# The latent gate's two GEMMs between the latents' projections, norms and queries of a two-block kernel; the first convolution's GEMM inside the attention loop

## What is computed

```python
z, xbc, dt_raw, q_a, c_kv, k_rope, gate_ssd, gate_mla = split_cols(u @ w_in[i], IN_SPLITS)
y_ssd = ssd_branch(z, xbc, dt_raw, ...) @ w_ssd_out[i]      # begins with a causal convolution of xbc and a SiLU
y_mla = mla_branch(q_a, c_kv, k_rope, ...) @ w_mla_out[i]   # latent attention, 16 heads
merged = jax.nn.sigmoid(gate_ssd) * y_ssd + jax.nn.sigmoid(gate_mla) * y_mla
```

```python
q = (rms_norm_2(q_a, q_a_norm) @ w_q_b).reshape(b, s, MLA_HEADS, QK_HEAD_DIM)
kv = (rms_norm_2(c_kv, kv_a_norm) @ w_kv_b).reshape(b, s, MLA_HEADS, QK_NOPE_DIM + V_HEAD_DIM)
```

## Time and profile before

| quantity | value |
|---|---|
| median of 3 runs | 1200.77 us (1197.71 to 1200.79) |
| the profiled execution's own time | 1201.91 us |
| its span in the trace | 1199.8 us |
| mean granted TensorE clock in it | 0.945 of full |
| PE busy | 1058.1 us, 88% of the span |
| POOL, DVE, ACT busy | 651.6, 532.0, 428.1 us |

### The profile page before, as it was taken

The page is one execution under the profiler, slowest core; times in us unless marked ns, Lnnn a source line. Parts: engine busy times, 40 slices in busy tenths (PEclk is TensorE's granted clock), DMA queues, the critical chain, the costliest instruction groups (busy, mean ns, idle before and its releaser), DMA issues.

```text
span 1199.8 us, 18315 instructions
## 1 busy us (share of the span) xinstructions
PE 1058.1 (88%) x7022; PEld 865.8 (72%) x7022; DVE 532.0 (44%) x1199; ACT 428.1 (36%) x641; POOL 651.6 (54%) x535
## 2 busy tenths in 40 slices
PE   5897899987957979999999999999985899999990
PEld 4786888987947879999976879898964555544440
DVE  6303246368545665644169886841226311111113
ACT  4543333332325546554434444354422211111111
POOL 5997814356738676664755359888540122322221
PEclk9999898999987889999998999999997999999996
DMA  6454522333424344432433226555425699999983
GB/s 255 174 200 166 183 71 71 113 117 123 141 105 142 139 141 141 141 137 75 164 126 102 100 72 212 175 176 175 176 105 246 219 417 418 417 417 419 418 338 110
DMA packets 35598, 229.05 MB, mean 191 GB/s; under 512 B 6320, under 2 KB 6320, under 8 KB 8768
## 3 DMA queue, kind: packets, MB, share of 16 engines
q1 hardware_dynamic: 30672, 220.07, 48.9%
q0 software_dynamic: 3696, 4.21, 1.1%
q10 hardware_dynamic: 1152, 3.67, 0.9%
HBM read 246.79 MB, written 11.27 MB: 215 GB/s over the span
## 4 chain that ended last, share of the span: by engine, by line
POOL 44%; issue 31%; DMA 11%; PE 11%; DVE 3%; POOLq 1%; ACT 0%; DVEq 0%
POOL wlo L516 44%; DMA ring<-in_experts 10%; PE ps L2320 5%; PE ps L2334 3%; DMA yg<-expert_rows,posn 1%; PE ps L2307 0%; PE ps L2282 0%; PE ps L1744 0%; PE ps L2283 0%; PE ps L1746 0%; PE ps L1745 0%; DVE xlo L983 0%; POOLq L519 0%; DVE over L1703 0%; DVE x L1718 0%
## 5 line engine op out<-in xcount | busy, mean ns | idle before, releaser
L516 POOL TENSOR_TENSOR wlo<-raw,whi 128x512 fp32r<-128x512 f32 x448 | 583.5, 1338 | 308.4 <-ACT whi L574 307.9
L1794 PE MATMUL ps<-xhi,whi 128*128 128x256 f32 x960 | 283.8, 296 | 10.5 <-DVE xlo L1200 4.1
L1795 PE MATMUL ps<-xhi,wlo 128*128 128x256 f32 x960 | 277.9, 289 | 0.0
L1796 PE MATMUL ps<-xlo,whi 128*128 128x256 f32 x960 | 277.7, 289 | 0.0
L574 ACT ACTIVATE whi<-raw 128x2048 fp32r<-128x2048 f32 x112 | 213.9, 1914 | 146.9 <-PE ps L1796 75.5
L1794 PEld LDWEIGHTS ps<-xhi,whi 128*128 128x128 f32 x960 | 191.3, 199 | 14.7 <-issue 7.2
L1795 PEld LDWEIGHTS ps<-xhi,wlo 128*128 128x128 f32 x960 | 190.9, 199 | 1.0 <-issue 0.7
L1796 PEld LDWEIGHTS ps<-xlo,whi 128*128 128x128 f32 x960 | 190.7, 199 | 0.0
L2320 PE MATMUL ps<-ring,xw 128*64 128x256 f32 x1248 | 152.6, 385 | 8.4 <-DMA ring<-in_experts 6.2
L2320 PEld LDWEIGHTS ps<-ring,xw 128*64 128x64 f32 x1248 | 86.8, 137 | 69.0 <-issue 29.5
L541 POOL DMA_INDIRECT expert_rows<-yb,dest x39 | 38.6, 989 | 172.4 <-ACT yb L900 172.4
(11 more groups left out here) (451 smaller groups left out, 1435.3 us busy)
## 6 DMA issues: line engine op xcount, KB each, us to landing
ring<-in_experts SPq DMA_DIRECT2D x117, 1024.0 KB
raw<-in_weights SPq DMA_DIRECT2D x112, 1024.0 KB, 4.9
x<-in_x SPq DMA_DIRECT2D x2, 512.0 KB, 4.6
memt<-in_mem ACTq DMA_DIRECT2D x1, 1024.0 KB, 6.1
out<-xn ACTq DMA_DIRECT2D x4, 256.0 KB, 2.5
expert_rows<-yb,dest POOLq DMA_INDIRECT x39
decay<-in_decay ACTq DMA_DIRECT2D x1, 512.0 KB, 3.6
npost<-in_norm_post ACTq DMA_DIRECT2D x1, 512.0 KB, 5.1
```

Of the source, the lines that this page charges most:

```text
L516: ins = pool.tensor_tensor(wlo[:, j, c], raw[:, j, c], whi[:, j, c].bitcast(f32), ALU.subtract)
L1794: mm(o_, wh[:, k, cc], hi[:, k0 + r0 + k, :], start=first, stop=False, skip_group_check=True)
L1795: mm(o_, wl[:, k, cc], hi[:, k0 + r0 + k, :], start=False, stop=False, skip_group_check=True)
L1796: ins = mm(o_, wh[:, k, cc], lo[:, k0 + r0 + k, :], start=False, stop=last, skip_group_check=True)
```

## The change

`gm0` and `gm1` move from the end of the attention's filler to the stretch behind `pb`: PE runs `gm0` (two units) ahead of the wait for `qa_ready`, and `gm1` (two units) behind the transposes of `ck` and `kp`. `xbc0` leaves that stretch and becomes the first two units of the filler, which now has twelve units (u from 0 to 11) and nothing behind the loop. The convolution's instructions of ACT and DVE move one odd or even iteration on, so that `conv_taps(5)` stands in u = 11 and `conv_silu(5)` in u = 12. `pa` and `pb` get another place in SBUF, since the gate's result `gmT` now exists while they do. No instruction is added or removed.

```diff
@@ unit_plan
     add("pb", w, 1024, r(5536, 5824))
-    add("xbc0", w, 1024, r(2048, 2560))
+    for i in range(2):
+        add(f"gm{i}", w, 1024, r(6848 + 512 * i, 7360 + 512 * i))
...
-    for i in range(1, 6):
+    for i in range(6):
         add(f"xbc{i}", w, 1024, r(2048 + 512 * i, 2560 + 512 * i))
-    for i in range(2):
-        add(f"gm{i}", w, 1024, r(6848 + 512 * i, 7360 + 512 * i))
@@ ACT
+            hi_upto(UNIT["gm0"][0] + 2)
+            hi_upto(UNIT["gm0"][1] + 2)
+            latent_gate(0)
             hi_parts("qa", 3, 8, D("g_qa"))
-            hi_upto(UNIT["xbc0"][0] + 2)
             hi_parts("ck", 2, 11, D("g_ckv"))
-            hi_upto(UNIT["xbc0"][1] + 2)
-            conv_first(0)
+            hi_upto(UNIT["gm1"][0] + 2)
+            hi_upto(UNIT["gm1"][1] + 2)
+            latent_gate(1)
...
-                if u < 10 and u % 2:
-                    conv_first(u // 2 + 1)
-                if u % 2 == 0 and u <= 10:
-                    conv_tanh(u // 2)
-                if u == 11:
-                    latent_gate(0)
-            hi_upto(MLA_FILL[13] + 2)
-            latent_gate(1)
+                if u < 12 and u % 2:
+                    conv_first(u // 2)
+                if u % 2 == 0 and 2 <= u <= 12:
+                    conv_tanh(u // 2 - 1)
@@ DVE
-            conv_taps(0)
...
-                if u < 10 and u % 2:
-                    conv_taps(u // 2 + 1)
-                if u % 2 == 0 and u <= 10:
-                    conv_silu(u // 2)
+                if u < 12 and u % 2:
+                    conv_taps(u // 2)
+                if u % 2 == 0 and 2 <= u <= 12:
+                    conv_silu(u // 2 - 1)
@@ PE
             gemm("pb", tm, xhi, xlo)
+            gemm("gm0", fm, xhi, xlo)
             pe.wait_ge(sem("qa_ready"), 2)
             transposes("qa", 3, lambda t, c: pa[:, t, 32 + c * P:32 + c * P + P])
-            fm("xbc0", 0, xhi, xlo)
             pe.wait_ge(sem("ck_ready"), 2)
             transposes("ck", 2, tiles(pb))
...
-            fm("xbc0", 1, xhi, xlo)
+            gemm("gm1", fm, xhi, xlo)
...
-                if u < 13:
+                if u < 12:
                     fm(units[MLA_FILL[u]][0], units[MLA_FILL[u]][1], xhi, xlo)
...
-            fm("gm1", 1, xhi, xlo)
```

More of the change, by code:

```diff
@@ L168, in bank_plan @@
     gemm("pb")
+    gemm("gm0")
     G += [("qa", 0), ("qa", 1)]
-    gemm("xbc0")
+    gemm("gm1")
     for i in range(3):
@@ L174, in bank_plan @@
     gemm("vv", [("vv", j) for j in range(4)])
-    for n in ("xbc1", "xbc2", "xbc3", "xbc4", "xbc5", "gm0", "gm1"):
+    for n in ("xbc0", "xbc1", "xbc2", "xbc3", "xbc4", "xbc5"):
         gemm(n)
@@ L327, in program @@
         a = A
-        pa = at("pa", a, [P, TT, 416])
-        pb = at("pb", a + 3328, [P, TT, 288])
         gmT = at("gmT", a, [P, 8, S])
@@ L344, in program @@
         km = at("km", a, [P, 16, S])
+        pa = at("pa", a, [P, TT, 416])
+        pb = at("pb", a + 3328, [P, TT, 288])
         a += 16 * KB
@@ L459, in halves @@
                 v.scalar_tensor_tensor(lo[:, d, :], b3, 0.5, hi[:, d, :].bitcast(f32), ALU.mult, ALU.subtract).then_inc(sem(ready), 1)
-        MLA_FILL = [n for name in ("xbc1", "xbc2", "xbc3", "xbc4", "xbc5", "gm0", "gm1") for n in UNIT[name]]
+        MLA_FILL = [n for name in ("xbc0", "xbc1", "xbc2", "xbc3", "xbc4", "xbc5") for n in UNIT[name]]
         block = ctx.enter_context(nc.Block())
@@ L714, in conv_tanh, with latent_gate @@
                     act.activation(xbc[:, 4 * i + 2 * j:4 * i + 2 * j + 2, :], cv[:, j, :, :], ACT.Tanh).then_inc(sem("conv_tanh"), 1)
+            def latent_gate(i):
+                for j in range(2):
+                    c = 4 * i + 2 * j
+                    release(tanh_half((f"gm{i}", j), gmT[:, c:c + 2, :]), (f"gm{i}", j))
             for name, dst, w, junk, stat_, c0 in (("pa", pa, 416, 0, "qa", 32), ("pb", pb, 288, 384, "ck", 0)):
@@ L742, in _ @@
             hi_upto(UNIT["vv"][0] + 2)
-            def latent_gate(i):
-                for j in range(2):
-                    c = 4 * i + 2 * j
-                    release(tanh_half((f"gm{i}", j), gmT[:, c:c + 2, :]), (f"gm{i}", j))
             copy(("mQ", 0), qmT[0:96, 0, :], rows=slice(0, 96))
```

## The result

The changed kernel takes 1208.96 us (median of 17 runs, 1207.43 to 1215.07) against 1199.48 us for the kernel before (17 runs on the same chip, 1196.04 to 1207.57): ratio 1.008, 95% interval 1.0068 to 1.0091, thus some 9.5 us slower: less than 1%, but clear of the noise. The prediction was +6.7 us, 1207.5 us. The profiled execution took 1207.47 us with a span of 1205.3; the one before took 1201.91 with 1199.8.

The account below looks back on a forecast made before the run. The prediction took PE, busy 88% of the span, as the bound and asked where it stands still. Its terms, 9.4 - 0.2 - 2.5 = +6.7 us, took the median from 1200.77 to 1207.5 us; range 1202 to 1212.5.

Parts of the forecast that it names:

- First part: From the end of `pb` to `wq0`: 34.6 us for four units against 25.2 for two, +9.4 us.
- Rival A: Key-value latent's roots ahead of `ck` run beside busy POOL: +4.3 us more, +11.0 in sum, 1211.8 us; chance 0.13.
- my 1.7: In `gm1`, behind the gap ahead of `ck`: four us at half speed, costing 1.7 us.
- the bound of +12: Upper bound for `pb` to `wq0`: `gm0` and `gm1` both at half speed for some us.
- Second part: From `wq0` to the twelfth filler unit: `wq2`'s weights come some 0.2 us earlier, -0.2 us.
- Third part: From the twelfth unit's end to `ym0`: two units fewer, but DVE's taps delay the maxima; -2.5 us, bounds -5.9 and -1.0.
- the two ends: Attention tail up to `ym0`: 5.9 us saved at full clock, only 1.7 if all runs at half speed.
- Rival B: Clock stays up in both new gaps, ahead of `ck` and in the tail: +1.6 us, 1202.4 us; chance 0.19.
- Rival C: Not slower: taps hidden in the tail, saving 10.6 us there, clock up in front; -3.1 us, 1197.7 us; chance 0.08.

Follow-up runs that it names:

- the taps in halves: The changed kernel with the last convolution's taps taken out of u = 11 and done in two halves in u = 13 and 14; 1207.55 us, ratio 1.0054.
- spare matmuls: The changed kernel plus 54 matmuls with unused results where PE waits in the attention's tail; 1207.76 us, ratio 1.0069.
- The repetition: The changed kernel once more with no edit, for a second trace; 1209.41 us.
- the tail alone: The kernel before with its own front, `gm0` behind it, twelve filler units and the last taps still in u = 9; 1208.03 us, ratio 1.0052.

## Why the prediction was right, and where its sum was not

The direction and the mechanism held, and the forecast median of 1207.5 us lies 1.5 below the measured one. As a difference it is less close, +6.7 against +9.5, since the forecast started from a median of 1200.77 and the later runs of the kernel before gave 1199.48. Some of it is luck as well: by stages the sum is off by +1.5, -1.1 and +1.9 us, and the -1.1 isn't the change's doing. Step by step:

**First part, +9.4, measured +10.9.** `gm0` started 2.3 us behind `pb`, ended by POOL's `wlo`: as said. The wait for `qa` was gone: as said. POOL stopped at 397.4, 0.6 us ahead of the roots, which took 2.5 us; gap ahead of `ck` 5.15 against 5.3. Rival A (the roots meet POOL) would have shown pairs of 2.4 us, as they still stand ahead of `pa`; it didn't come, in no trace of this front. `gm1` took 13.5 us (402.40 to 415.9) against 11.7 at full clock, 1.8 for my 1.7. The roots, then, go by POOL and not by their place in the program: 2.5 us with a pair at 0.35 us in a new place with POOL idle, and 6.7 us again where a later version runs them beside POOL. The Trainium skill (SBUF — State Buffer, "Who interferes with whom") says that a DVE instruction with two SBUF inputs contends with a GpSimd instruction that reads SBUF, and these traces agree.

The step that failed: I gave `gm0` full clock, and had its loss only in the bound of +12. It had 0.59 over 383 to 387 us, and took 13.1 us from 382.13 to 395.24, 1.4 more than 11.7; that is the missing part but for 0.1. PE had waited 2.14 us ahead of it. That wait alone doesn't settle the clock: one of the six traces with `gm0` ahead of `qa`, that of the taps in halves, had the same wait and kept 1.00 over 380 to 400 us, and its front is 1.6 us shorter (34.5). The loss in `gm1` isn't fixed either: with spare matmuls the front took 34.9, since `gm1` took 12.3 us (402.80 to 415.1).

**Second part, -0.2, measured -1.3.** Up to the queries it is -0.4. The other -0.9 is in the loop, and goes with the clock. In the first 7 us behind the queries' transposes PE had these granted clocks, in the kernel before and in the changed one:

```profile
437.10:444.10 7.00, 6.12 (x28) 5.59 (x29) 3.10 (x6) 2.90 (x7) 0.00 (x0) 0.50 0.42 150
446.00:453.00 7.00, 6.12 (x35) 5.60 (x36) 3.10 (x6) 2.88 (x7) 0.00 (x0) 0.63 0.40 150
```

From the queries to the twelfth unit's end it took 96.9 and 96.0 us. The repetition, with 0.62, took 96.1; the six other traces of the table, with 0.50 to 0.54, took 96.6 to 97.5. So this -0.9 looks like a difference of clocks between runs, and not like a gain of the change.

**Third part, -2.5, measured -1.4 up to `ym0`, and -0.6 up to `acum`,** since `ym0` begins at the low level. The order of events is as written: the maxima of head 13 behind the taps, done at +7.9 (predicted +8.0), those of head 14 at +11.1 (+11.4). Then the sum fails at a named step: "maxima of head 14 to +11.4, exponentials to +12.5, transposes, copy and the last outputs". There is a head 15. I took the last maxima for those of head 14. That round costs 2.0 us at full clock (555.27 to 557.28 in the kernel with spare matmuls) and 3.5 at the low level (552.53 to 556.01). Against it I had counted the low level with 4.2 us where it costs about 2.9 up to `ym0` (23.6 against 20.7 with spare matmuls). So the two ends should have been -4.3 at full clock and -1.4 at the low level instead of -5.9 and -1.7, and the time came out at the second one: I chose a middle, and all of the tail ran near the low level (0.59).

That choice was the weakest. I argued with PE's share of busy time, and took PE to be busy half of the time. It was busy 21.2 of 25 us by the trace, partly because at the low level it is busy longer with the same matmuls, and the clock was low all the same. Two stretches kept 1.00 with no more: 544 to 551 us of the kernel before, busy 5.85 of 7, and the tail alone, busy 12.5 of 16.5 us (545.2 to 561.7). The busy share of a stretch doesn't tell the two apart.

**Rival B** (clock up in both places, +1.6) fell: the low level cost 1.8 us in `gm1`, 1.4 in `gm0` and 3.7 in the tail, 6.9 in sum. The kernel before lost 3.3 us in the same stages, in its two `xbc0` units, and some 0.9 more than the changed one at the loop's begin. So my estimate is that 2.7 of the 9.0 us (6.9 - 3.3 - 0.9) are clock. The Trainium skill (TensorE: Matmul & The Clock Gate, "What's actually happening") says that the slow starts are under 1% of a typical span and advises not to fit a model to them. The 6.9 us are 0.6% of this span, which agrees, but they are most of the effect's size, so here they can't be left out. **Rival C** (not slower) named the right condition for the tail. With the taps out of the tail and the clock up, the stretch to `ym0` took 16.5 us, a saving of 8.5 where C has 10.6. But the change puts the taps there, and the front costs 10.9 us more anyhow.

What stays open: why the granted clock differs between runs of equal code, which moved the end of `pb` by up to 7 us, and which part of the medians' 9.5 us it makes.

## What to carry to other kernels

Filling a gap with work only pays the part of the gap that is there without the work: here 11.7 us of GEMM went into a stretch whose real slack was 6.1 us, and opened a new gap behind it, because another engine's chain (DVE's lower parts and roots) could start only when PE had done the filler and the transposes behind it. When filler is taken from the end of a loop, write down head by head, to the last one, what each other engine does in the iterations that are now bare, and keep blocks such as five us of taps out of them. Look for a gap that depends on nothing that you move: the one ahead of the rotated queries took a unit for nothing, and was worth 6 us. Compare single traces by stages, with each stage's granted clock beside its length.

## What the runs showed of the hardware

Three things were not expected. First, a run of two-input DVE instructions beside a run of POOL instructions went one of two ways. In the changed kernel they took turns, 12 rotations in 16.8 us:

```profile
429.11 1.15 DVE L992 TENSOR_TENSOR ropetmp<-qm,ropt 128x256 f32<-128x256 f32 x1 [20.44 <-ACT qm L592]
430.19 1.51 DVE L993 TENSOR_TENSOR ropetmp<-qm,ropt 128x256 f32<-128x256 f32 x1
```

With the same instructions in front (the kernel with spare matmuls) the first one waited until POOL stopped:

```profile
428.32 14.82 DVE L992 TENSOR_TENSOR ropetmp<-qm,ropt 128x256 f32<-128x256 f32 x1 [19.26 <-ACT qm L592]
443.06 0.41 DVE L993 TENSOR_TENSOR ropetmp<-qm,ropt 128x256 f32<-128x256 f32 x1
```

All twelve took 18.9 us, and PE waited 7.9 us for the queries instead of 5.8. Which way it goes is not set by the code up to there: the changed kernel, its repetition and the taps in halves took turns. Second, PE's mean granted clock was 0.59 over 25 us in which PE was busy for 21.2 by the trace, in small matmuls with gaps of 1 to 2 us; with 54 more matmuls in those gaps it was 1.00, and the stretch to `acum` 3.7 us shorter. Third, the same 365 matmuls took 47.8 us at a granted clock of 1.00 and 50.7 at 0.93 in two runs of one kernel.
